# RWKV chunk inverse: four levels on compact 32-column blocks in a TensorE loop, the last level by four 32x32 tiles

## The reference

```python
def wkv7_scan(S0, r, w, k, v, a, b):
    def step(S, inp):
        r_t, w_t, k_t, v_t, a_t, b_t = inp
        sa = jnp.einsum('bhvk,bhk->bhv', S, a_t)
        S = S * w_t[:, :, None, :] + sa[..., None] * b_t[:, :, None, :] + v_t[..., None] * k_t[:, :, None, :]
        return S, jnp.einsum('bhvk,bhk->bhv', S, r_t)
```

## Time and profile before

| | us |
|---|---|
| median of 3 runs (2460.64 to 2466.29) | 2464.23 |
| span of the profiled execution | 2464.6 |
| PE busy | 2401.6 (97%) |
| PEld busy | 1958.3 |
| DVE busy | 1628.6 |
| ACT busy | 1278.5 |
| POOL busy | 236.4 |
| L1282 PE matmul, 2560 records, busy | 88.8 |
| L1294 PE matmul, 2560 records, busy | 83.6 |

### The profile page before, as it was taken

How to read it: one execution, slowest core, us unless ns; L and a number is a source line. 1 busy time by engine, 2 the same in 40 slices (tenths; PEclk the granted TensorE clock), 3 DMA queues, 4 the chain that set the end, 5 groups by cost and what they waited for, 6 DMA issues and landing times.

```text
span 2464.6 us, 48665 instructions
## 1 busy us (share of the span) xinstructions
PE 2401.6 (97%) x20666; PEld 1958.3 (79%) x20666; DVE 1628.6 (66%) x1792; ACT 1278.5 (52%) x1368; POOL 236.4 (10%) x212
## 2 busy tenths in 40 slices
PE   8999998999999999999999989999999999999998
PEld 4677576888886577877777878888888888888887
DVE  2544876222334956555666378888888888888887
ACT  4322025222222744543444277777777777777774
POOL 2000642000000322211122000000000000000000
PEclk8999999999999899999999999999999999999999
DMA  7566126333224201111110379999999999999993
GB/s 267 186 230 231 52 86 171 86 102 93 95 96 152 66 15 32 32 32 32 32 32 29 113 275 370 337 365 340 364 338 367 338 364 339 368 336 363 346 359 135
DMA packets 249096, 490.79 MB, mean 199 GB/s; under 512 B 14616, under 2 KB 107568, under 8 KB 248624
## 3 DMA queue, kind: packets, MB, share of 16 engines
q1 hardware_dynamic: 247214, 481.42, 55.1%
q10 hardware_dynamic: 1730, 7.10, 0.8%
HBM read 486.40 MB, written 2.10 MB: 198 GB/s over the span
## 4 chain that ended last, share of the span: by engine, by line
PE 92%; DVE 4%; ACT 1%; issue 1%; DMA 1%; SPq 0%; POOL 0%; ACTq 0%; DVEq 0%
PE bank L1604 25%; PE bank L1631 12%; PE bank L1141 3%; PE bank L1142 3%; PE bank L1143 3%; PE bank L1282 3%; PE bank L1294 3%; PE bank L1255 2%; PE bank L1047 2%; PE bank L1018 2%; PE bank L1019 2%; PE bank L1020 2%; PE bank L1159 2%; PE bank L1158 2%; PE bank L1160 2%; PE bank L884 1%
## 5 line engine op out<-in xcount | busy, mean ns | idle before, releaser
L2945 DVE TENSOR_TENSOR w_low<-expert_w,w_high 128x1792 fp32r<-128x1792 f32 (+2 forms) x384 | 769.1, 2024 | 124.9 <-ACT w_high L2154 123.5
L2154 ACT CAST w_high<-expert_w 128x1792 fp32r<-128x1792 f32 (+2 forms) x384 | 654.1, 1704 | 245.4 <-PE bank L1604 153.0
L1604 PE MATMUL bank<-w_high,xg_high 128*128 128x448 f32 x1024 | 294.1, 369 | 4.0 <-DVE xg_low L2935 4.0
L1604 PE MATMUL bank<-w_low,xg_high 128*128 128x448 f32 x1024 | 291.5, 366 | 0.0
L1604 PE MATMUL bank<-w_high,xg_low 128*128 128x448 f32 x1024 | 291.5, 366 | 0.0
L1604 PEld LDWEIGHTS bank<-w_high,xg_high 128*128 128x128 f32 x1024 | 191.3, 189 | 20.1 <-DVE xg_low L2935 4.2
L1604 PEld LDWEIGHTS bank<-w_low,xg_high 128*128 128x128 f32 x1024 | 193.0, 189 | 15.5
L1604 PEld LDWEIGHTS bank<-w_high,xg_low 128*128 128x128 f32 x1024 | 192.9, 188 | 15.3
L1631 PE MATMUL bank<-w_high,hid_high 128*128 128x512 f32 x448 | 175.3, 391 | 0.0
L1631 PE MATMUL bank<-w_high,hid_low 128*128 128x512 f32 x448 | 174.5, 389 | 0.0
L1631 PE MATMUL bank<-w_low,hid_high 128*128 128x512 f32 x448 | 174.3, 389 | 0.0
(11 more groups left out here) (421 smaller groups left out, 4243.8 us busy)
## 6 DMA issues: line engine op xcount, KB each, us to landing
expert_w<-in_moe_w_dram SPq DMA_DIRECT2D x192, 1792.0 KB, 9.3
arena<-in_mod_w_dram SPq DMA_DIRECT2D x48, 1024.0 KB, 8.1
arena<-in_ffn_w_dram SPq DMA_DIRECT2D x44, 512.0 KB, 5.1
arena<-in_hy_w_in_dram SPq DMA_DIRECT2D x12, 1024.0 KB, 5.3
arena<-in_rw_w_rkv_dram SPq DMA_DIRECT2D x48, 256.0 KB, 2.8
arena<-in_ffn_w_dram SPq DMA_DIRECT2D x11, 1024.0 KB, 4.9
arena<-in_hy_w_out_dram SPq DMA_DIRECT2D x4, 1024.0 KB, 9.3
arena<-in_rw_w_out_dram SPq DMA_DIRECT2D x8, 512.0 KB, 3.6
```

Of the source, the lines that this page charges most:

```text
L1604: last = pe.matmul(bank[b0 + v][:, 0:EH], x[:, k, :], w_[:, kk, v * EH:v * EH + EH], start=(k == 0 and x is XGH and w_ is wh), stop=(k == ...
L2154: act.copy(high_piece(kind, n), piece(kind, ering[q % ERN], n // 2, n % 2))\
L2945: dve.tensor_tensor(piece(kind, low[s], n // 2, n % 2), piece(kind, ering[s], n // 2, n % 2), high_piece(kind, n).bitcast(F32), ALU.subtract)\
```

## The change

The first four levels (block sizes 1 to 16 solved, joined to 2 to 32) need only the 32x32 blocks on the diagonal of each 64x64 matrix. So TM, YP and a new TN (TM turned) become 8 blocks by 32 columns; the partition says which of the two diagonal blocks a value belongs to. The first merge takes the even and the odd blocks out of the 64-column scores in two steps. Each half of a level is 32 products of 32x32x32 on the four diagonal tiles of the array, and the four levels with two halves for two heads are the body of a loop `pe.Fori(0, LOOPED)` with waits on register values. All filler of TensorE moves behind the loop. The last level computes only the off-diagonal 32x32 blocks, 16 products for each half and head. ScalarE spreads TN over the 64-column TT with zeros off the diagonal (two activations with a scale of 1 or 0 by partition), and VectorE merges the last result into it. On VectorE `finish` and `ahead_bonus` move behind the levels and `ahead_key_raw` behind the inverse; on POOL `next_digits` waits for the last turn of the loop, and the unit blocks come before the key square. Elsewhere three waits on an engine's own result take another semaphore.

```diff
+            def level_first(h, count):
+                pe.wait_ge(sem("level_turned"), count)
                 settle(pe)
                 for x in range(2 * NB):
+                    for j in range(4):
+                        q, cs = slice(HC * j, HC * j + HC), slice(HC * (j % 2), HC * (j % 2) + HC)
+                        last = mm(bank[h][q, x * HC:x * HC + HC], AB[h][q, x, cs], TN[h][q, x, :], start=True, stop=True)
+                last.then_inc(sem("level_products"), 1)
+
+            def level_second(h, count):
+                pe.wait_ge(sem("level_copied"), count)
                 settle(pe)
                 for x in range(2 * NB):
+                    for j in range(4):
+                        q = slice(HC * j, HC * j + HC)
+                        last = mm(bank[2 + h][q, x * HC:x * HC + HC], YP[h][q, x, :], TM[h][q, x, :], start=True, stop=True)
+                last.then_inc(sem("level_products"), 1)
+
+            def last_first(h, i):
+                pe.wait_ge(sem("level_turned"), PER_PAIR * i + 2 * LOOPED + h + 1)
...
+                            x, near_, far = d * NB + b, C * s_ + HC * d, C * s_ + HC * (1 - d)
+                            r = slice(far, far + HC)
+                            last = mm(bank[h][near_:near_ + HC, x * HC:x * HC + HC], AB[h][r, x, HC * d:HC * d + HC],
+                                      TN[h][r, x, :], start=True, stop=True)
...
+                for h in range(2):
+                    step(pe, "pair_copies", f"score_copy_{h}", i)
+                    step(pe, "pair_vectors", f"keys_masked_{h}", i)
+                settle(pe)
+                with pe.Fori(0, LOOPED) as lv:
+                    for h in range(2):
+                        level_first(h, lv * 2 + (PER_PAIR * i + h + 1))
+                    for h in range(2):
+                        level_second(h, lv * 2 + (PER_PAIR * i + h + 1))
                 step(pe, "pair_vectors", "out_masked_1", i)
                 for d in range(2):
                     turn(4 + d, Bt[d]).then_inc(sem("pair_products"), one("pair_products", f"b_turned_{d}"))
-                first_half(1, 0, i)
                 step(pe, "pair_copies", "a_copy_1", i)
+                for d in range(2):
+                    turn(6 + d, Kt[d]).then_inc(sem("pair_products"), one("pair_products", f"k_turned_{d}"))
+                for h in range(2):
+                    last_first(h, i)
                 step(pe, "pair_copies", "b_copy_1", i)
                 turn(5, Vf).then_inc(sem("pair_products"), one("pair_products", "v_turned"))
+                for h in range(2):
+                    last_second(h, i)
                 z(0)
                 z(1)
                 step(pe, "ahead_vectors", "bonus_in", i)
                 mm(bank[5][:, 0:SEQ], heads1, KD, start=True, stop=True)\
                     .then_inc(sem("pair_products"), one("pair_products", "bonus_sum"))
                 if more:
+                    ahead_keys(i + 1, range(KT))
                     ahead_decay(i + 1)
                     ahead_rate(i + 1)
...
+                def turn_level(h):
+                    dve.transpose(TN[h].rearrange("p b c -> p (b c)"), TM[h].rearrange("p b c -> p (b c)"))\
+                        .then_inc(sem("level_turned"), 1)
...
+                def join(lv, h):
+                    dve.wait_ge(sem("level_products"), level_product(i, lv - 1, 1, h))
+                    settle(dve)
+                    dve.copy_predicated(by_dir(TM[h], HC), each_block(level_bits[lv - 1]),
+                                        by_dir(bank[2 + h][:, 0:2 * NB * HC], HC))\
...
+                    turn_level(h)
```

More of the change, by code:

```diff
@@ L148, in constants, with near @@
     reset = [np.tile(pos != 0, (P, 1)), np.tile(pos != C - 1, (P, 1))]
-    layer1 = np.concatenate([*keys_mask, *out_mask, *reset, row == chunk_col], 1)
-    bits = np.concatenate([level(b, a) for b in (1, *LEVELS) for a in (True, False)] +
+    even = i[:, None] // HC % 2 == 0
+    def near(b, after_rows):
+        r, c = i[:, None] % HC, np.arange(HC)[None, :]
+        pair = r // (2 * b) == c // (2 * b)
+        r2, c2 = r // b % 2, c // b % 2
+        return pair & (r2 == 1) & (c2 == 0) if after_rows else pair & (r2 == 0) & (c2 == 1)
+    layer1 = np.concatenate([*keys_mask, *out_mask, *reset, row == chunk_col,
+                             i[:, None] % HC == np.arange(HC)[None, :], even, ~even], 1)
+    bits = np.concatenate([near(1, a) & which for which in (even, ~even) for a in (True, False)] +
+                          [near(b, a) for b in LEVELS for a in (True, False)] +
                           [level(C // 2, False), level(C // 2, True)], 1)
@@ L512, in build @@
         near_at = mark()
-        AB, YP, TM = ([sb(2 * NB, C) for _ in range(2)] for _ in range(3))
+        AB = [sb(2 * NB, C) for _ in range(2)]
+        YP, TM, TN = ([sb(2 * NB, HC) for _ in range(2)] for _ in range(3))
         keys_at = mark()
@@ new lines, in last_second @@
+            def last_second(h, i):
+                pe.wait_ge(sem("level_copied"), PER_PAIR * i + 2 * LOOPED + h + 1)
+                settle(pe)
+                for b in range(NB):
+                    for d in range(2):
+                        for s_ in range(2):
+                            x, q = d * NB + b, slice(C * s_ + HC * d, C * s_ + HC * d + HC)
+                            at_ = x * C + HC * (1 - d)
+                            last = mm(bank[2 + h][q, at_:at_ + HC], TM[h][q, x, :], YP[h][q, x, :], start=True, stop=True)
+                last.then_inc(sem("level_products"), 1)
@@ L2017, in first_copy @@
                 def first_copy(lv, h):
[L2018 to L2020 removed]
+                    act.wait_ge(sem("level_products"), level_product(i, lv, 0, h))
+                    act.copy(YP[h].rearrange("p x c -> p (x c)"), bank[h][:, 0:2 * NB * HC]).then_inc(sem("level_copied"), 1)
                 def z_copy(h):
@@ L2035, in pair @@
                         .then_inc(sem("pair_copies"), one("pair_copies", f"a_copy_{d}"))
-                first_copy(0, 0)
-                first_copy(0, 1)
+                for lv in range(LOOPED):
+                    for h in range(2):
+                        first_copy(lv, h)
                 for d in range(2):
@@ new lines, in first_join @@
+                def first_join(h):
+                    step(dve, "pair_products", f"scored_{h}", i)
+                    step(dve, "pair_pool", f"eye_{h}", i - 1)
+                    settle(dve)
+                    scores = bank[h][:, :].rearrange("p (d b c) -> p d b c", d=2, c=C)
+                    for j, name in enumerate(("joined_even", "joined_0")):
+                        dve.copy_predicated(by_dir(TM[h], HC), each_block(first_bits[j]), scores[:, :, :, HC * j:HC * j + HC])\
+                            .then_inc(sem("pair_vectors"), one("pair_vectors", f"{name}_{h}"))
+                        step(dve, "pair_vectors", f"{name}_{h}", i)
+                    turn_level(h)
@@ L2789, in pair @@
                 dve.tensor_copy(DC, DCn).then_inc(sem("pair_vectors"), one("pair_vectors", "chunk_decay"))
-                for lv in range(1, 5):
+                for lv in range(1, LOOPED + 1):
                     for h in range(2):
-                        joined(lv, h)
-                if more:
-                    ahead_key_raw(i + 1)
+                        join(lv, h)
+                if i:
+                    finish(i - 1)
+                ahead_bonus(i)
                 step(dve, "pair_products", "bonus_sum", i)
```

159 lines of the change are left out of this document (52 added, 107 removed).

## The result

The changed kernel takes 2447.25 us (median of 4 runs, 2442.24 to 2449.69), the kernel before 2463.29 in the same comparison: ratio 0.9932, 95% interval 0.9918 to 0.9946. A later comparison on another chip gave 2448.36 (5 runs) and 0.9934 [0.9921, 0.9947]. The forecast was 2447.0.

What follows compares the result with a forecast made beforehand. TensorE, busy 97%, bounds the kernel; loop 12.6 + code 2.5 + register waits 0.5 + rest 16.2 = 31.8 us against 33.8 in seven pairs, 3.0 less in the last: 17 us together, 2447 us; 8 in 10 from 2430 to 2484.

Steps and rivals of the forecast that it cites:

- Group of 0.5 us: In the level loop, 64 matmul records on four 32x32 tiles at once take 0.5 us, against 0.93 before.
- Rival 2: In the level groups, tiles no quicker: 14.5 ns a record, groups of 0.93 us, total 2476 us; 13%.
- A level of 3.3 us, the last 2.7: One level in the loop takes 3.3 us end to end, the loop's last 2.7 for TensorE; loop 12.6 us.
- First pass with 2.5 us for code and 0.5 for register waits: Loop's first pass waits 2.5 us a pair for code (0 to 5); register waits and branches add 0.5 (0 to 2).
- rival 1: Code and branches eat the gain: first pass waits 4.5 us, not 2.5, total 2463 us; 15%.
- Clock at full: Between the scores and the turns the granted clock stays at 1.00; a lower one would prove the forecast wrong.
- rival 3: The clock falls in the loop and the turns behind it: about 4.5 us a pair, total 2484 us; 9%.
- After the loop 16.2 us: From the loop's last product: turns, last level, z, bonus, keys, 0.9 us wait for key_copy, decay and rate, 16.2 us.
- Last pair 24.5: Last pair, without keys, decay and rate: stretch of 24.5 us against 27.5, 3.0 less.
- Code blocks, 9 a pair instead of 11: Queue q8 brings about 9 code blocks a pair, fewer than 11; blocks in later passes would prove the forecast wrong.
- Rival 4: Loop body fetched again on each pass: loop 31 us, 13 us a pair slower, total 2568 us; 6%.
- Rival 5: In the level groups, a record never under 29 ns on average: groups of 1.86 us, total 2567 us; 3%.

## Why the prediction was right, point by point

The total was right to 1 us: 17 us predicted, 16 to 17 measured. The mechanism is the predicted one: less work for TensorE in the levels, paid for with waits inside the loop. That the sum fits so closely is luck, since errors of about 1 us a pair stood against each other. No run separates the 32-column levels from the packing of the filler behind them or from the smaller last level; their shares are read from the trace.

- **Group of 0.5 us**: measured 0.63 (64 records at 9.9 ns). This is the term that was mis-sized. I took 58 ns for a tile, halved it with the columns and divided by four. The single tile follows the columns (32 ns), but in turn records start 9.9 ns apart, and with 64 columns 14: half the columns save 29%, not half. Rival 2 put its border at about 11 ns, and 9.9 is nearer to that than to my 7.6.
- **A level of 3.3 us, the last 2.7**: 3.38 and 2.83 at full clock (pass starts above). Both groups of a head lie on its chain, so 0.26 us should have come on top. Three rows of pass 3, between the products at 1203.40, 1204.80 and 1206.78, show what took it back:

```profile
1204.21 0.37 ACT L2033 COPY arena<-bank 128x256 f32<-128x256 f32 x1 [2.35 <-PE bank L1297]
1205.70 0.45 DVE L2791 COPY_PREDICATED arena<-arena,bank 128x256 f32<-128x256 int32 x1 [1.64 <-PE bank L1306]
1206.18 0.45 DVE L2774 STREAM_TRANSPOSE arena<-arena 128x256 f32<-128x256 f32 x1
```

  From the start of a group the copy comes after 0.81 us and the merge after 0.90, which is 0.18 and 0.27 behind the group's 0.63; I had taken 0.27 and 0.37 from the 64-column level, and 0.28 from the copy to the second half where it is 0.22. The work itself was as forecast: copy 383 ns, merge 424 and transpose 446, against 370, 430 and 430.
- **First pass with 2.5 us for code and 0.5 for register waits**: 6.3 predicted, 50.8/8 = 6.35 measured. The wait is 1.9 to 2.6 us in six pairs and, as two waits, 4.3 and 4.0 in pairs 3 and 6, which is near the size of rival 1; a cost of register waits is not to be seen beside it. The mechanism as I told it, blocks fetched in series behind the scores, was incomplete: the block's transfer starts only as TensorE nears its end of the code, so work ahead of the loop hid little of it.
- **Clock at full**: wrong, and one of the prediction's own signs against itself. This was rival 3, at 9%, and it is there in every pair, but small: about 0.7 us in pass 2 ((32.4 - 8 x 3.38)/8), not 4.5. In the last step of its argument I had the whole loop and the turns at half clock; by the windows the fall lasts some 3.4 us in five of the pairs, 7 in two and 10 in one, and the chain through the other engines does not slow with TensorE.
- **After the loop 16.2 us**: 15.0 to 15.6. Its own terms, 12.95 + 0.9 + 1.06 + 1.06, give 16.0; the 0.2 has no source. z starts 4.0 us after the loop instead of 4.7, because v_copy is through by then (it ended at 1213.46, z started at 1213.60). The bonus took 0.35, not 0.6. The wait for key_copy came as predicted, 0.77 against 0.9.
- **Last pair 24.5**: 24.7. **Code blocks, 9 a pair instead of 11**: 109 in all instead of 125, which is that. One of the 9 comes in pass 2, which the prediction had named as a sign against itself; but TensorE does not wait for it, and passes 3 and 4 bring none.
- **Nothing moves elsewhere**: scores to first level product 5.9 us in most pairs, as before; wu to the next scores 28.3 to 28.9 in six of seven, and before 28.5 to 28.8 in as many.

So the sum came out because 0.9 us too much behind the loop stood against 1.1 too little in it. Rival 4, the body fetched again on each pass, is refuted by passes 2 to 4 at 3.38 us; the unrolled loop shows what it would have cost. Rival 5 is refuted by the 9.9 ns.

## What to carry to other kernels

Before small tiles multiply the instructions of TensorE, count blocks of code. In this kernel straight code got one block, some 125 matmuls with their weight loads, per 3.5 to 4 us; a loop body paid once, with a wait inside its first pass that work moved ahead of the loop hid only in small part. Halving the columns of a product on four tiles saved 29% of its time and doubled the code; halving the count of products was worth more (32 us). And read the wait rows after a move: the 0.8 us for a copy that lost its cover was predicted, and one reordered product took it back.

## What the runs showed of the hardware

- fp32 records of 32x32 in a row on one tile start 32 ns apart at full clock and 53 at half; on four tiles in turn 9.9 ns apart, with 64 columns 14.
- A body of 512 instructions shows no idle under issue over 0.33 us in passes 2 to 4; written out, the same passes stop 0.9 to 2.4 us at every block.
- TensorE went on 1.2 to 1.6 us after the end of the transfer of the block that it waited for in the loop of the changed kernel.
- The clock fell to 1.2 GHz during a wait of 1.2 to 2.8 us for code or within 2.3 us after it, in all eight pairs. With waits of at most 0.8 us and longer records no fall began in any of the eight loops, and with a wait of 0.73 us and the same records none in either of two. It was also at 1.2 GHz for most of a stretch in which one tile after the other was recorded busy throughout.
